# Two seven-product pairs in three feed-forward stages, and weight-sum blocks loaded through ScalarE's queue

## The reference

```python
def swiglu(x, w_in, w_out):                      # stages 0 to 3; stage 4 has w_gate, w_up, w_down apart
    gate, up = jnp.split(x @ w_in, 2, axis=-1)   # x: 256 x 1024, w_in: 1024 x 5632
    return (jax.nn.silu(gate) * up) @ w_out      # w_out: 2816 x 1024
...
x = x + 0.5 * swiglu(rms_norm(x, ffn1_norm_g[i]), ffn1_w_in[i], ffn1_w_out[i])
```

## Time and profile before

| what | value |
|---|---|
| median of 3 runs (range) | 1527.47 us (1527.09 to 1528.89) |
| the profiled execution | 1527.58 us, its span 1525.9 us |
| granted TensorE clock | 0.999 |
| busy share of the span | PE 99%, PE weight loads 84%, DVE 73%, ACT 57%, POOL 17% |
| read from HBM | 295.92 MB, 195 GB/s over the span |

### The profile page before, as it was taken

One profiled execution on the slowest core, in us unless ns is written; L12 is line 12 of the kernel. 1 busy time (PEld: TensorE's weight loads), 2 busy tenths in 40 slices (PEclk: granted clock), 3 DMA queues, 4 the chain that ended last, 5 costly groups with the idle time before them and its releaser, 6 DMA issues.

```text
span 1525.9 us, 19569 instructions
## 1 busy us (share of the span) xinstructions
PE 1515.7 (99%) x7714; PEld 1281.9 (84%) x7714; DVE 1110.0 (73%) x1211; ACT 867.3 (57%) x1087; POOL 263.8 (17%) x216
## 2 busy tenths in 40 slices
PE   9999999999999999999999999999999999999998
PEld 7888888888888888888888888899988888888886
DVE  6687766556787568776776788599998568667875
ACT  7545554646455554556776455476887344454554
POOL 0222200001132122220001232100571000012220
PEclk9999999999999999999999999999999999999999
DMA  7997656446976699765416975666554665579762
GB/s 253 308 262 222 188 173 200 138 166 217 276 219 195 182 289 259 217 188 179 151 56 213 305 226 185 207 190 203 180 182 145 215 193 188 174 219 302 211 185 101
DMA packets 274307, 311.40 MB, mean 204 GB/s; under 512 B 64272, under 2 KB 233512, under 8 KB 274216
## 3 DMA queue, kind: packets, MB, share of 16 engines
q1 hardware_dynamic: 273112, 308.84, 65.4%
q10 hardware_dynamic: 1104, 1.31, 0.3%
HBM read 295.92 MB, written 1.09 MB: 195 GB/s over the span
## 4 chain that ended last, share of the span: by engine, by line
PE 94%; issue 2%; DVE 2%; ACT 1%; POOL 1%; DMA 1%; ACTq 0%; DVEq 0%; POOLq 0%
PE ps L2371 24%; PE ps L2375 24%; PE ps L2372 24%; PE ps L2413 3%; PE ps L2587 2%; PE ps L2588 2%; PE ps L2586 2%; PE ps L2361 2%; PE ps L2363 2%; PE ps L2362 2%; PE ps L2414 1%; PE ps L2429 1%; PE ps L2542 1%; DMA scr<-in_mem_dram 1%; PE ps L2693 0%
## 5 line engine op out<-in xcount | busy, mean ns | idle before, releaser
L1411 DVE TENSOR_TENSOR w_lo<-w_raw,w_hi 128x2048 fp32r<-128x2048 f32 x250 | 592.0, 2372 | 175.4 <-ACT w_hi L793 175.1
L793 ACT ACTIVATE w_hi<-w_raw 128x2048 fp32r<-128x2048 f32 x250 | 477.1, 1912 | 229.0 <-PE ps L2375 210.0
L2371 PE MATMUL ps<-w_hi,xg 128*128 128x512 f32 (+1 forms) x960 | 375.0, 391 | 0.0
L2375 PE MATMUL ps<-w_hi,xg 128*128 128x512 f32 (+1 forms) x960 | 372.1, 388 | 0.0
L2372 PE MATMUL ps<-w_lo,xg 128*128 128x512 f32 (+1 forms) x960 | 372.0, 387 | 0.0
L2371 PE MATMUL ps<-w_hi,y_hi 128*128 128x512 f32 x666 | 261.6, 393 | 0.5 <-DVE w_lo L1418 0.2
L2375 PE MATMUL ps<-w_hi,y_lo 128*128 128x512 f32 x666 | 259.1, 389 | 0.0
L2372 PE MATMUL ps<-w_lo,y_hi 128*128 128x512 f32 x666 | 258.9, 389 | 0.0
L761 POOL COPY scr<-scr 128x512 uint16<-128x512 uint16 x100 | 112.8, 1144 | 778.9 <-DVE scr L1526 778.9
L2371 PEld LDWEIGHTS ps<-w_hi,xg 128*128 128x128 f32 x960 | 180.3, 188 | 37.2 <-issue 0.7
L2375 PEld LDWEIGHTS ps<-w_hi,xg 128*128 128x128 f32 x960 | 180.2, 188 | 37.0
(11 more groups left out here) (409 smaller groups left out, 1864.1 us busy)
## 6 DMA issues: line engine op xcount, KB each, us to landing
w_raw<-in_ffn_w_in_dram SPq DMA_DIRECT2D x168, 512.0 KB, 4.9
w_raw<-in_ffn_w_out_dram SPq DMA_DIRECT2D x88, 512.0 KB, 4.8
w_raw<-in_w_in_dram SPq DMA_DIRECT2D x82, 512.0 KB, 4.5
w_raw<-in_a_w_in_dram SPq DMA_DIRECT2D x28, 512.0 KB, 4.6
w_raw<-in_w_down_dram SPq DMA_DIRECT2D x22, 512.0 KB, 4.5
w_raw<-in_w_gate_dram SPq DMA_DIRECT2D x21, 512.0 KB, 4.0
w_raw<-in_w_up_dram SPq DMA_DIRECT2D x21, 512.0 KB, 5.0
y_raw<-in_ffn_w_in_dram SPq DMA_DIRECT2D x16, 512.0 KB, 5.4
```

Of the source, the lines that this page charges most:

```text
L793: act.activation(w_hi[:, u % RING, :], w_raw[:, u % RING, :], ACT.Copy).then_inc(w_rounded, 1)
L1411: dve.tensor_tensor(w_lo[:, s, :], w_raw[:, s, :], w_hi[:, s, :].bitcast(F32), ALU.subtract).then_inc(w_split, 1)
L2371: pe.matmul(dst, xh, hi, start=start, stop=False, skip_group_check=True)
L2375: return pe.matmul(dst, xl, hi, start=False, stop=stop, skip_group_check=True)
```

## The change

`PAIR` is replaced by `PAIRS_OF`: one pair in stages 0 and 1, now of tiles 8 and 9, and two pairs in stages 2, 3 and 4, of tiles 4, 5 and of 8, 9. `ffn_places` counts the units' places. The half blocks leave SP's queue: ACT issues all of them, those of a stage's first pair in the steps from five tiles ahead of it on (before `silu(0, 0)`, in step 1 and in step 2, where the first pair is 4), those of a second pair inside the first one's `pair`. The sums of weights for a first pair move from four steps into the two steps ahead of the pair, those for a second pair into the end of the first `pair` and step 7. The sums of x are used by both pairs. The last hidden values may now be turned inside `pair`.

```diff
+PAIRS_OF = ((8,), (8,), (4, 8), (4, 8), (4, 8))
...
+def ffn_places(pairs):
+    order, i = [("G", 0, 0), ("G", 0, 1)], 1
+    while i < NI:
+        if i in pairs:
+            order += [("G", i, 0), ("G", i, 1), ("G", i + 1, 1), ("D", i - 1), ("G", i + 2, 0), ("G", i + 2, 1), ("D", i), ("D", i + 1)]
+            i += 3
+        else:
+            order += [("G", i, 0), ("G", i, 1), ("D", i - 1)]
+            i += 1
+    return {step: k for k, step in enumerate(order + [("D", NI - 1)])}
...
-                    sp.dma_start(dst, part).then_inc(t_landed[k], 16)
...
+                def block(p, k):
+                    half, i = ((0, p), (0, p + 1), (1, p + 1), (1, p))[k]
+                    if p == pairs[0]:
+                        act.wait_ge(w_used, u + 1)
+                    else:
+                        act.wait_ge(pe_done, pe_.at(f"M{(5, 7, 6, 4)[k]} {f} {pairs[0]}"))
+                    for j in range(2):
+                        dst = t_raw[k].rearrange("p (k c) -> p k c", k=4)[:, :, 256 * j:256 * j + 256]
+                        act.dma_start(dst, gu_src(f, half, i)[j]).then_inc(t_landed[k], 16)
+
+                def blocks(i):
+                    if i + 5 == pairs[0]:
+                        block(i + 5, 0)
+                    if i + 4 == pairs[0]:
+                        block(i + 4, 1)
+                        block(i + 4, 2)
+                    if i + 3 == pairs[0]:
+                        block(i + 3, 3)
...
+                def step(i):
+                    v = u + at["G", i, 0]
                     round_(v + 2)
                     hidden_high(i - 1, (i - 1) % 2)
-                    if i == 4:
-                        t_high(T1, f"T1 {f}")
-                    if i == 5:
+                    blocks(i - 1)
+                    if i + 1 == pairs[0]:
+                        t_high(i + 1, T2, "T2")
+                    if i + 1 in pairs[1:]:
+                        t_high(i + 1, T1, "T1")
+                    round_(v + 3)
+                    if i + 2 == pairs[0]:
                         s_high()
-                    round_(v + 3)
...
+                    t_high(p, T4, "T4")
+                    hidden_high(p - 1, (p - 1) % 2)
+                    if p + 4 in pairs:
+                        block(p + 4, 0)
+                        block(p + 4, 2)
...
+                blocks(-1)
                 silu(0, 0)
                 round_(u + 3)
                 silu(0, 1)
```

More of the change, by code:

```diff
@@ L346, in build, with alone_until, alone @@
         T1, T3, T2, T4 = range(4)
+        def alone_until(f, i):
+            def alone(f, j):
+                return j not in PAIRS_OF[f] and j - 1 not in PAIRS_OF[f]
+            return sum(alone(g, j) for g in range(f) for j in range(NI)) + sum(alone(f, j) for j in range(i + 1))
         x_sum = tiles(KB(40, 8))
@@ L545, in ffn @@
                     small_inputs()
[L546 to L575, removed]
+                i = 1
+                while i < NI:
+                    if i in pairs:
+                        pair(i)
+                        i += 3
+                    else:
+                        step(i)
+                        i += 1
+                if NI - 3 not in pairs:
+                    down(NI - 1)
                 if f == 4:
@@ L1655, in ffn @@
                     pass
-                for i in range(3, PAIR):
-                    step(i)
-                pair()
-                for i in range(PAIR + 3, NI):
-                    step(i, last=i == NI - 1)
+                i = 3
+                while i < NI:
+                    if i in pairs:
+                        pair(i)
+                        i += 3
+                    else:
+                        step(i)
+                        i += 1
             def mem(n, gain, factor):
@@ L2630, in gates @@
+                    pe.wait_ge(vec_done, vec.at(f"C21 {f} {p}"))
+                    gates(p + 2)
+                    down(p)
+                    down(p + 1, hidden=(lambda: hidden(NI - 1)) if p + 2 == NI - 1 else None)
                 def gates(i, first=None):
[L2632 to L2635 removed]
+                    gate_up(u + at["G", i, 0], 0, first=first)
+                    gate_up(u + at["G", i, 1], 1)
@@ L2638, in ffn @@
                         pe.wait_ge(act_done, act_.at("M kT 1"))
-                    down(i - 1, start=i == 1)
-                pair()
-                for i in range(PAIR + 3, NI):
-                    gates(i, taken(i - 1))
-                    down(i - 1, hidden=(lambda: hidden(NI - 1)) if i == NI - 1 else None)
+                    down(i - 1, start=i == 1, hidden=(lambda: hidden(NI - 1)) if i == NI - 1 else None)
+                i = 1
+                while i < NI:
+                    if i in pairs:
+                        pair(i)
+                        i += 3
+                    else:
+                        step(i)
+                        i += 1
                 down(NI - 1, norm=n + 1)
```

309 lines of the change are left out of this document (164 added, 145 removed).

## The result

The changed kernel takes 1538.14 us (median of 4 runs, 1535.79 to 1539.35), the kernel before on the same chip 1527.64 (1527.09 to 1528.89): a ratio of 1.0067, 95% interval 1.0052 to 1.0082. It is 10.5 us slower where 5.6 us faster was forecast.

The account below looks back on a forecast made before the run. PE, running without a gap, was taken as the bound, its matmul count setting the time. 1527.58 less 8.16 saved plus 2.7 of waits gave 1522.1, or 1522.0 us on the median's scale, range 1519.0 to 1526.0.

Parts of the forecast that it names:

- The saving: Stages 2 to 4: one more pair each, 36 matmuls fewer at 0.2267 us, 8.16 us saved.
- I take 0.46, the row of ACT's own queue: Openings of stages 2 to 4: each DMA issue on ACT takes 0.46 us, four in step 1 take 1.84.
- an issue as slow as SP's slowest: Rival, chance 0.03: ACT issues take 1.51 us, costing 5.5 to 6 us a stage, 17 in all, 1536.
- These edits I cost at nothing: First pair of stages 2 to 4, and steps 6 and 7: added work fits under cover, at no cost.
- The openings: Stages 2 to 4 from D(0) on, without cover: waits of 0.9 us a stage, 2.7 us in three.
- The rule weighed: Stage openings: DMAs from several engines share 16 DMA engines, so ACT's queue gains transfers nothing and blocks meet hidden's transpose.
- the upper end of one term: Step 1 of stages 2 to 4: D(1) waits up to 1.2 us, where 0.3 was taken.
- ACT issues ahead of its waiting activations: Rival, chance 0.15: step 1's blocks go out early and delay D(0) 2.2 us a stage, 6.6 in all, 1526.0.
- No wait at all: Rival, chance 0.27: packed order fits and queues are quick, so PE never waits, 1519.4 us.
- larger waits, 1.5 to 3 us a stage: Rival, chance 0.10: the forecast's waits in stages 2 to 4 are there but larger, 1524 to 1528.
- The slower one: Rival, chance 0.03: ACT issues as slow as SP's slowest, 1.51 us; decides against the change from about 1.0 us, 1536.
- Both signs of being wrong: Waits in step 7 or at C21 from late T sums; an ACT issue above 0.7 us.

Follow-up runs that it names:

- e16: The change with step 1's blocks spread, second pair's T2 block later, x sum halved, transpose before a load, T1's sum behind G(2,1)'s split: 1524.23 us, 0.9978 of the kernel before.
- e3: The changed kernel with the half blocks of steps 1 and 2 issued behind the step's two silu: 1535.09 us, 1.0046 of the kernel before.
- e5: The changed kernel with one block of step 1 beside hidden_high(0) and the other behind the step's two silu: 1533.37 us, 1.0031 of the kernel before.
- e2: The changed kernel with the pair at tile 4 alone in stages 2 to 4: 1542.01 us, 1.0096 of the kernel before.
- e4: The changed kernel with three of the second pair's blocks issued some 20 us later: 1555.59 us, 1.0187 of the kernel before.
- e6: e5 with the second pair's block for T2 also issued some 7 us later: 1530.88 us, 1.0021 of the kernel before.
- e1: The changed kernel with one pair at tile 8 alone in all five stages: 1528.67 us, 1.0001 of the kernel before.
- e8: The changed kernel with the large sum over x moved ahead of hidden_low(0) in stages 2 to 4: 1533.71 us, 1.0035 of the kernel before.
- e7: e6 with e8's edit, the large sum over x ahead of hidden_low(0): 1529.92 us, 1.0012 of the kernel before.
- e10: The changed kernel with all half blocks issued on SP's queue: 1547.80 us, 1.0131 of the kernel before.
- e15: e7 with x sum halved, T1's sum early, T2's block in step 2, and hidden(1)'s transpose ahead of G(3,0)'s load: 1530.31 us, 1.0006 of the kernel before.

## Why the prediction was wrong

**The saving was right.** 36 x 0.2267 = 8.16. e16's profiled execution is 3.3 us below that of before and still loses 5.1 from D(0) to the ends of the three stages, 8.4 together; some four tenths of the saving were had.

**"I take 0.46, the row of ACT's own queue": the step that failed first.** The row was of issues at the start of the program, with little under way. Four in step 1 took 3.0 to 4.2 us, so 0.76 to 1.05 each, for the forecast's 0.46. I had the bound: SP's slowest of 1.51 in the earlier trace rows. I took "an issue as slow as SP's slowest" as a rival at 0.03, and worked out that it decides against the change from 1.0 us on. The right question was what is under way when the fourth is issued. e3 and e5 show that this costs G(2,0) its 3.6 us and part of D(1)'s wait (3.1 us in three stages, 2.6 in e3, 2.1 in e5).

A second slip lies in the same sum. It held the end of the split (5.1) against G(2,0)'s 5.44, but PE is released by `product(1)`, which stands behind the split and which the same paragraph has ending at 5.9. With the 4.8 us from the rounding to G(2,0), a rounding at 0.9 would itself have made G(2,0) some 0.2 us late: the lead that the forecast saw there did not exist.

**"These edits I cost at nothing": the second pair.** I counted VectorE's time in the first pair, which did fit. I did not price the 3 MB that it now shares with the weight units. The unit for G(6,1) landed up to 11.7 us behind its issue, and through rounding, snapshot and C21 that reached PE; in e2, e4 and e6, which have fewer blocks or none beside that load, the wait is gone. With what follows it the second pair cost 5.5 us of the 8.2. I had named C21 as a place where waits would refute me, for another cause (late sums of weights).

**The openings were a sum of small margins, each taken on its own.** D(0) didn't wait, as forecast, and D(1) and the low parts did, but for longer. G(2,1) and D(2), where I took 0.3, never waited; G(2,0), where I took 0, lost 3.6 in three stages. The sum was 2.7 us and is 16.3. Issues 1.2 to 2.4 us longer than forecast made G(2,0) late and shifted VectorE's row, which in stage 2 had no idle time left from G(2,0)'s split to the middle of the pair. A part of D(1)'s wait goes with them; the low parts' waits stayed in e3 and e5, so that they come from the long issues isn't shown. The matmul behind each gap starts some 0.1 late again, 2.6 us in all, which I hadn't in the sum.

**The rule weighed bears on more than one term.** Share and rate of the 16 DMA engines over step 1 of stage 2 in the changed kernel, and over the first pair's blocks (columns as in the earlier trace rows):

```profile
547.00:562.00 15.00, 13.29 (x60) 10.68 (x59) 7.28 (x6) 6.88 (x6) 4.58 (x3) 1.00 1.02 340
...
601.00:616.00 15.00, 14.77 (x64) 11.54 (x64) 14.47 (x11) 7.66 (x7) 0.77 (x2) 1.00 1.05 337
```

The same stretches of the kernel before:

```profile
546.00:561.00 15.00, 15.00 (x68) 12.40 (x67) 9.54 (x7) 7.00 (x6) 2.52 (x3) 1.00 1.07 307
...
598.00:613.00 15.00, 15.00 (x68) 12.43 (x67) 10.41 (x7) 5.84 (x7) 5.89 (x3) 1.00 0.85 216
```

In the pair the share rose from 0.85 to 1.05. In step 1 it was as high before (1.07, at 307 GB/s for 340), without a gap on PE; so a full share by itself doesn't cost, it depends on what stands behind what. The Trainium skill (DMA: Bandwidth & Descriptors, Issuing engines are not separate DMA queues) says that DMAs of several issuing engines interleave on the same 16; by that rule the loads and transposes on SP's queue are slowed by blocks on ACT's, and e4 (a transpose of 8.9 us for 3.1) agrees. I had kept it for the upper end of one term only.

**The rivals.** "ACT issues ahead of its waiting activations" falls: the blocks of step 1 start at 549.15, `hidden_high(0)` at 549.14. (Its price in the prediction doesn't add up either: 1.3 MB at 350 GB/s are 3.7 us, not 2.4.) "No wait at all" and "larger waits, 1.5 to 3 us a stage" fall. The slower one had the nearest mechanism and time (1536), but the long issues make 3.6 us of the 16.3 at G(2,0), and 5.7 with all that e5 mends.

**What was to show it.** From D(0) (1369.14) to the pair (1409.8) in stage 4 are 40.7 us, so 2.6 of waits for the forecast's 0.9 a stage. `turn_back(0)`'s `join` came 3.2 behind its issue: the first block doesn't disturb it, as forecast. No waits in stages 0 and 1: right, and e1 confirms it for the pair at 8. Both signs of being wrong came: waits at C21, 2.7 us in three stages, and issues on ACT above 0.7 us, up to 2.24.

## What to carry to other kernels

Where PE runs without a gap, price a moved transfer like an instruction: ask what else is under way when it is issued, which load or transpose lands behind it, and whose in-order row stands behind that. A DMA issue read in a quiet stretch (0.46 us here) says little of one in a full stretch (up to 2.24). Ask which wait ends last at each place, and test the sum there. And a margin of 0.3 to 1.6 us can be spent once: when several engines' rows are filled at the same time, add the lateness along the chain before taking each place's small wait.

Such a loss can often be got back without giving up the saving: five small moves took the change from +10.5 to -3.4 us.

## What the runs showed of the hardware

**An issue is long where much is under way, but the number of transfers doesn't settle it.** In the changed kernel ScalarE's issues of half blocks with two to five transfers under way have medians of 0.37 to 0.53 us, and single ones reach 1.35. Of the six that met six, the two third ones of a row of four took 0.52, the four fourth ones 0.78, 1.50, 1.91 and 2.24. In e8 the fourth ones of stages 3 and 4 met six too, 1 us later, and took 0.86 and 0.68. Whether the length goes with all that is under way or with the issues on the same queue, no run separates. All of them in stages 0 to 3 (ns min/median/max):

```profile
L895 ACTq DMA_DIRECT2D y_raw<-in_ffn_w_in_dram x24: 374/389/1347, 95.3 to 903.1; - x24
L895 ACTq DMA_DIRECT2D scr<-in_ffn_w_in_dram x24: 374/525/2235, 113.6 to 922.5; - x24
```

**An issue doesn't wait for the activation ahead of it to end**, only for it to start (549.15 beside 549.14), and the activation behind waits for the issue (3.69 us "issue").

**VectorE and GpSimd hold each other up.** `join` takes 1.35 us alone and 2.36 beside the sum over x (e7; the sum ends at 549.15, the copy 1.2 us later), two `cut` 1.17 or 3.23. The other way round, D(1)'s split took 3.38 in stage 2 of the changed kernel, where a `join` had begun 0.6 us before it, for 2.29. The Trainium skill (SBUF — State Buffer, SBUF: two separate sides) describes a port pair shared by the two, taken by a VectorE operation with two SBUF inputs for its whole length; the trace agrees.

**The clock fell after some waits.** In e4 PE waited 3.03 us at 640.13, and from 641.1 to 644.1 matmuls started 0.43 apart in place of 0.23. Stretches ahead, in it and behind:

```profile
636.00:640.00 4.00, 1.09 (x5) 0.56 (x3) 0.86 (x1) 1.11 (x2) 2.40 (x3) 1.00 1.13 348
640.20:644.00 3.80, 3.80 (x10) 3.02 (x11) 2.53 (x2) 3.04 (x2) 0.00 (x0) 0.57 1.05 376
644.00:650.00 6.00, 6.00 (x27) 4.92 (x26) 5.87 (x3) 1.92 (x1) 0.00 (x0) 0.99 1.11 256
```

The granted clock of 0.57 is mostly the lower level, 1.2 GHz; eight matmuls at 0.20 more are 1.6 us on top of the wait. In e10, behind 3.4 us in stage 2, it was 0.50 for more than 5 us. In e15 it fell behind a wait of 2.0 us (the row above). None of the change's own waits, up to 1.9 us by starts, had this.
